# Splitting the last layer norm of a decoder layer over VectorE, ScalarE and GpSimd

## What is computed

```python
ALPHA = (2.0 * DEPTH) ** 0.25

def _layernorm(x, g, b):
    xf = x.astype(jnp.float32)
    mu = jnp.mean(xf, -1, keepdims=True)
    var = jnp.mean(jnp.square(xf - mu), -1, keepdims=True)
    return ((xf - mu) * lax.rsqrt(var + LN_EPS) * g + b).astype(x.dtype)
...
    x = _layernorm(ALPHA * x + (1 + g1) * (merged @ w_o), ln_mix_g, ln_mix_b)
    u2 = x * (1 + sc2) + sh2
    f = _hier_moe(u2.reshape(b * L, D), ...).reshape(b, L, D)
    x = _layernorm(ALPHA * x + (1 + g2) * f, ln_ffn_g, ln_ffn_b)
```

## Time and profile before

| | us |
|---|---|
| median of 3 runs | 2881.74 |
| lowest and highest of them | 2880.91, 2882.03 |
| the profiled execution | 2883.5 |
| its span, from the first to the last instruction | 2881.8 |
| TensorE busy | 2587.6 (90%) |
| VectorE busy | 1508.3 (52%) |
| ScalarE busy | 1051.6 (36%) |
| GpSimd busy | 425.4 (15%) |
| first landing of rows in the last stage | 2806.2 |
| last stage, from there to the end of the span | 75.6 |

### The profile page before, as it was taken

One profiled execution on the slowest core, in us unless ns is written; L12 is line 12 of the kernel. 1 busy time (PEld: TensorE's weight loads), 2 busy tenths in 40 slices (PEclk: granted clock), 3 DMA queues, 4 the chain that ended last, 5 costly groups with the idle time before them and its releaser, 6 DMA issues.

```text
span 2881.8 us, 34273 instructions
## 1 busy us (share of the span) xinstructions
PE 2587.6 (90%) x11876; PEld 1890.9 (66%) x11876; DVE 1508.3 (52%) x2374; ACT 1051.6 (36%) x1338; POOL 425.4 (15%) x261
## 2 busy tenths in 40 slices
PE   7999999999999976899999999999939999999970
PEld 2376666666666654677789998884427777777750
DVE  3332576766765767200012222115567888888869
ACT  0212645536446454200000000000017777777751
POOL 0000000000000001111034431110002233233220
PEclk8989999999999988899999999999959999999985
DMA  7721222222222211111111113121148999999963
GB/s 269 255 69 41 79 59 61 66 70 66 66 57 79 59 39 37 46 44 36 44 35 47 44 51 110 37 61 52 52 151 290 345 347 347 353 354 342 341 234 134
DMA packets 251191, 379.58 MB, mean 132 GB/s; under 512 B 17395, under 2 KB 167547, under 8 KB 251049
## 3 DMA queue, kind: packets, MB, share of 16 engines
q1 hardware_dynamic: 230272, 336.17, 35.3%
q0 software_dynamic: 11904, 26.15, 2.4%
q10 hardware_dynamic: 8928, 16.26, 1.8%
HBM read 356.21 MB, written 39.76 MB: 137 GB/s over the span
## 4 chain that ended last, share of the span: by engine, by line
PE 39%; issue 7%; DVE 6%; ACT 4%; DMA 2%; POOL 1%; DVEq 0%; ACTq 0%; POOLq 0%; SPq 0%
PE bank L1999 11%; PE bank L1961 5%; PE bank L1963 5%; PE bank L1962 5%; PE bank L2071 4%; ACT we_parts L1080 3%; PE bank L2135 2%; PE bank L2138 2%; PE bank L2139 2%; DVE we_parts L1574 1%; DMA rows_dram<-arena 1%; PE bank L2104 1%; DVE x_parts L1684 1%; ACT arena L1101 1%; PE bank L2145 1%
## 5 line engine op out<-in xcount | busy, mean ns | idle before, releaser
L1835 PE MATMUL bank<-u_whole,arena 128*128 128x344 f32 x2304 | 695.3, 458 | 0.0
L1835 PEld LDWEIGHTS bank<-u_whole,arena 128*128 128x128 f32 x2304 | 437.6, 193 | 221.6 <-issue 16.7
L1961 PE MATMUL bank<-u_parts,w_parts 128*128 128x344 f32 x960 | 313.8, 327 | 14.4 <-DVE u_parts L1434 7.3
L1574 DVE TENSOR_TENSOR we_parts<-u_whole,we_parts 128x2048 fp32r<-128x2048 f32 x129 | 295.1, 2287 | 57.5 <-ACT we_parts L1080 57.5
L1962 PE MATMUL bank<-u_parts,w_parts 128*128 128x344 f32 x960 | 308.6, 321 | 0.0
L1963 PE MATMUL bank<-u_parts,w_parts 128*128 128x344 f32 x960 | 308.5, 321 | 0.0
L1999 PE MATMUL bank<-arena 128*128 128x344 f32 x1056 | 307.8, 452 | 0.0
L1999 PEld LDWEIGHTS bank<-arena 128*128 128x128 f32 x1056 | 200.1, 190 | 101.8
L1080 ACT ACTIVATE we_parts<-u_whole 128x2048 fp32r<-128x2048 f32 x129 | 247.0, 1916 | 51.5 <-PE bank L2135 26.9
L2117 PE MATMUL bank<-we_parts,x_parts 128*128 128x512 f32 x512 | 210.0, 410 | 3.3 <-DVE we_parts L1574 1.9
L2119 PE MATMUL bank<-we_parts,x_parts 128*128 128x512 f32 x512 | 201.4, 393 | 0.0
(11 more groups left out here) (327 smaller groups left out, 3921.1 us busy)
## 6 DMA issues: line engine op xcount, KB each, us to landing
u_whole<-in_w_moe_dram SPq DMA_DIRECT2D x128, 1024.0 KB, 7.4
arena<-in_w_moe_dram SPq DMA_DIRECT2D x64, 1024.0 KB, 7.6
arena<-in_w_ada_dram SPq DMA_DIRECT2D x12, 2048.0 KB, 10.1
arena<-in_w_in_dram SPq DMA_DIRECT2D x48, 512.0 KB, 3.9
w_whole<-in_w_in_dram SPq DMA_DIRECT2D x40, 512.0 KB, 3.8
arena<-cum_dram ACTq DMA_DIRECT2D x62, 256.0 KB, 3.1
arena<-in_state_ssm_dram SPq DMA_DIRECT2D x16, 512.0 KB, 5.5
out_dram<-arena SPq DMA_DIRECT2D x16, 512.0 KB, 4.0
```

The lines of the kernel that those rows point to most:

```text
L1574: dve.tensor_tensor(w_los[v], wraw[slot], w_his[v].bitcast(F32), ALU.subtract).then_inc(wlo_ready, 1)
L1835: last = pe.matmul(banks[part][:, 0:SUB], wslot[u][:, k, :], uT[:, k, part * SUB:(part + 1) * SUB], start=(k == 0), stop=(k == KD - 1))
L1961: pe.matmul(out, w_hi[v][:, k, :], u_hi[:, k, at], start=(k == 0), stop=False)
```

## The change

The last three wide VectorE operations of a tile become three others. VectorE stops after mean and variance; later it works out two numbers for each row, 1 / std in `mv2[..., 3]` and - mean / std in `mv2[..., 0]` (`scale_of`). ScalarE applies them as scale and bias of one activation (`normed_rows`). GpSimd then multiplies with the weight row and adds the bias row, and raises `y_out`.

The order is set so: on VectorE, `scale_of(i - 1)` stands behind the combine of tile i; on ScalarE, `normed_rows(i - 1)` stands between the copy of tile i and its square root. The semaphores `mvar_ready` and `mstd_ready` are dropped, and `var_ready` and `std_ready` of the first normalisation are counted on; in the middle normalisation nothing else changes.

```diff
@@ gpsimd, behind its last scatter
+            pool.wait_ge(finw_landed, 64)
+            for i in range(TILES + 1):
+                rows = P if i < TILES else NS
+                x = fa[i % 3][0:rows, :]
+                pool.wait_ge(y_normed, i + 1)
+                st.did(pool.tensor_tensor(x, x, ffn_g[0:rows, :], ALU.mult))
+                st.settle()
+                pool.tensor_tensor(x, x, ffn_b[0:rows, :], ALU.add).then_inc(y_out, 1)
@@ scalar
+            def normed_rows(i):
+                rows = P if i < TILES else NS
+                act.wait_ge(scale_ready, i + 1)
+                act.activation(fa[i % 3][0:rows, :], fa[i % 3][0:rows, :], ACT.Identity, bias=mv2[0:rows, i % 2, 0:1],
+                               scale=mv2[0:rows, i % 2, 3:4]).then_inc(y_normed, 1)
+
             for i in range(TILES + 1):
...
                                scale=wts[0:rows, i:i + 1]).then_inc(f_scaled, 1)
-                act.wait_ge(mvar_ready, TILES + 2 + i)
+                if i >= 1:
+                    normed_rows(i - 1)
+                act.wait_ge(var_ready, 2 * TILES + 3 + i)
                 act.activation(mv2[0:rows, i % 2, 2:3], mv2[0:rows, i % 2, 1:2], ACT.Sqrt,
-                               bias=epsc[0:rows, :]).then_inc(mstd_ready, 1)
+                               bias=epsc[0:rows, :]).then_inc(std_ready, 1)
+            normed_rows(TILES)
@@ vector
+            def scale_of(i):
+                rows = P if i < TILES else NS
+                m = mv2[0:rows, i % 2, :]
+                dve.wait_ge(std_ready, 2 * TILES + 3 + i)
+                fin.did(dve.reciprocal(m[:, 3:4], m[:, 2:3]))
+                fin.settle()
+                dve.scalar_tensor_tensor(m[:, 0:1], m[:, 0:1], -1.0, m[:, 3:4], ALU.mult, ALU.mult).then_inc(scale_ready, 1)
+
             for i in range(TILES + 1):
...
                                                  ALU.mult, ALU.add))
+                if i:
+                    scale_of(i - 1)
                 fin.settle()
                 fin.did(dve.tensor_tensor(x, x, g2, ALU.mult))
...
                 fin.settle()
-                dve.bn_aggr(mv2[0:rows, i % 2, 0:2], stats2[0:rows, :]).then_inc(mvar_ready, 1)
-                dve.wait_ge(mvar_ready, TILES + 2 + i)
-                fin.did(dve.scalar_tensor_tensor(x, x, mv2[0:rows, i % 2, 0:1], ffn_g[0:rows, :], ALU.subtract,
-                                                 ALU.mult))
-                dve.wait_ge(mstd_ready, TILES + 2 + i)
-                fin.did(dve.reciprocal(mv2[0:rows, i % 2, 3:4], mv2[0:rows, i % 2, 2:3]))
-                fin.settle()
-                dve.scalar_tensor_tensor(x, x, mv2[0:rows, i % 2, 3:4], ffn_b[0:rows, :], ALU.mult,
-                                         ALU.add).then_inc(y_out, 1)
+                if i >= 2:
+                    dve.wait_ge(y_normed, i - 1)
+                dve.bn_aggr(mv2[0:rows, i % 2, 0:2], stats2[0:rows, :]).then_inc(var_ready, 1)
+            scale_of(TILES)
```

More of the change, by code:

```diff
@@ L379, in build @@
         x0_landed = [sem(f"x0_landed{i}") for i in range(2)]
-        wo_done, mvar_ready, mstd_ready, x0_used = sem("wo_done"), sem("mvar_ready"), sem("mstd_ready"), sem("x0_used")
+        wo_done, x0_used = sem("wo_done"), sem("x0_used")
         u2_ready, u2_turned, u2t_ready, logits_done = (sem("u2_ready"), sem("u2_turned"), sem("u2t_ready"),
@@ L399, in build @@
         f_scaled, y_out = sem("f_scaled"), sem("y_out")
+        scale_ready, y_normed = sem("scale_ready"), sem("y_normed")
         y_stored = [sem(f"y_stored{i}") for i in range(3)]
@@ L1051, in _ @@
                 rows = P if i < TILES else NS
-                act.wait_ge(mvar_ready, i + 1)
+                act.wait_ge(var_ready, TILES + 2 + i)
                 act.activation(mv2[0:rows, i % 2, 2:3], mv2[0:rows, i % 2, 1:2], ACT.Sqrt,
-                               bias=epsc[0:rows, :]).then_inc(mstd_ready, 1)
+                               bias=epsc[0:rows, :]).then_inc(std_ready, 1)
                 act.wait_ge(u2_turned, i + 1)
@@ L1526, in _ @@
                 st.settle()
-                dve.bn_aggr(mv2[0:rows, i % 2, 0:2], stats2[0:rows, :]).then_inc(mvar_ready, 1)
-                dve.wait_ge(mvar_ready, i + 1)
+                dve.bn_aggr(mv2[0:rows, i % 2, 0:2], stats2[0:rows, :]).then_inc(var_ready, 1)
+                dve.wait_ge(var_ready, TILES + 2 + i)
                 st.did(dve.scalar_tensor_tensor(x, x, mv2[0:rows, i % 2, 0:1], mix_g[0:rows, :], ALU.subtract,
                                                 ALU.mult))
-                dve.wait_ge(mstd_ready, i + 1)
+                dve.wait_ge(std_ready, TILES + 2 + i)
                 st.did(dve.reciprocal(mv2[0:rows, i % 2, 3:4], mv2[0:rows, i % 2, 2:3]))
```

## The result

The changed kernel takes 2892.14 us (median of 6 runs, 2889.89 to 2892.98) where the kernel before takes 2880.01 (median of 6 runs, 2874.90 to 2882.03). The ratio is 1.0043, with a 95% interval of 1.0030 to 1.0056, which is +8.6 to +16.1 us: slower, by 12.1 us. The forecast was +8.9.

What follows compares the result with a forecast made beforehand. The last stage was taken as bound by VectorE, nine tiles one behind the other at 8.0 us a turn. Start -0.9, turns +4.5 and tail +5.3 summed to +8.9 us: 2890.6 us against a median of 2881.74, range 2887 to 2898.

Steps and rivals of the forecast that it cites:

- The exclusion: Last stage: a GpSimd operation and a VectorE operation with two SBUF inputs exclude each other; handover gives back 0.14 us.
- The first rival: Last stage: GpSimd's multiplication gets ahead and holds the residual; turn 9.4 us, +15.2 us, 2896.9; chance 0.18.
- the narrow margin: Last stage: the residual is ready only 0.07 us ahead of GpSimd's multiplication, so their order could flip.
- GpSimd's 2.35 us: Last stage: each wide GpSimd operation with two full inputs takes 2.35 us, two a tile; lower end 1.89.
- The fourth rival: Last stage: exclusion, but 1.89 us for each GpSimd operation; loads bind at 8.05 a tile, +3.5 us, 2885.2; chance 0.07.
- The statistics: Last stage: VectorE's statistics, with one SBUF input, run free beside GpSimd's multiplication at 1.29 us.
- The second rival: Last stage: statistics are held by GpSimd too; turn 9.6 us, +17.5 us, 2899.3; chance 0.04.
- The turn: Last stage, one tile: 8.63 us against 8.0, combine held by GpSimd's addition; +4.5 us over seven turns.
- the cover of the loads: Last stage: late loads stay hidden behind the held combine by 0.24 us; loads half a microsecond longer add 1 us.
- Start and tail: Last stage: to the second residual's end -0.9 us; last residual to last addition 9.5 us for 4.2, +5.3.
- The store behind it is the same.: End of kernel: the store after the last addition is unchanged, so nothing is added there.
- The third rival: Last stage: nothing excludes anything; VectorE's turn 7.1 us until loads bind at 8.0, +2.5 us, 2884.2; chance 0.07.

## Why the prediction was right, step by step

**The exclusion** was there, and in the order that was forecast. The residual came ahead of the multiplication, by 0.18 us in seven of the eight tiles (0.29 in the first) and not 0.07: the ScalarE pass takes 1.24 us and not 1.13 as the copy. The first rival, which lived on the narrow margin, was further off than I thought. What did not hold is that the combine is held in every turn: with three buffers it was in two of seven, and by 0.27 us in a third. Nor does the exclusion alone decide the sign: without it, with four buffers, the stage was still 2.6 us longer than before. The Trainium skill, "ScalarE: Activation LUTs", section "What ACT_TABLE_LOAD costs", gives about 93 ns more for each pointer operand; the new pass has a pointer bias that the copy hasn't, and the 0.11 us between them are near to it.

**GpSimd's 2.35 us** measured 2.34 (2.33 on 8 rows). The fourth rival, with 1.89, is out.

**The statistics** stayed at 1.29 us beside the multiplication. The second rival is out, and the rule that the prediction cites from the Trainium skill for operations with one SBUF input agrees with this.

**The turn** of 8.63 measured 8.69, but for two causes that happened to add up. With loads out of the way it is 8.36, less than my 8.63: the reciprocal started before the combine's end and the narrow operation took 0.16 and not 0.23. And the cover of the loads, which I gave as 0.24 us, wasn't there: the copy at 2824.94 started 5.2 us after its loads were issued at 2819.72, and the next four copies 4.7 to 5.1 us after theirs, where I had taken 4.4. I had counted the landing from the first of the two issues, but the second is issued some 0.4 us later, and took up to 4.8 by itself. This term was mis-sized, by 0.3 to 0.8, and it changed what sets the turn: in four of the seven the combine waited for rows (8.6 to 9.4 us a turn), in three the exclusion set it (8.3 to 8.4). That the mean came out near 8.63 is luck.

**Start and tail**, -0.9 and +5.3, measured -1.0 and +5.1.

**What failed** is one sentence: "The store behind it is the same." The store is, but the program doesn't end with it. It ends when each engine has drained, and GpSimd, which had been done 83 us before the end, had become the last one. Those 5.2 us are missing from the sum: with them the forecast of the stage would have been +14.1, and it measured +14.2. Over whole runs the change measured +12.1, with an interval of +8.6 to +16.1. The +8.9, the +14.1 and the +14.2 all lie in it, +8.9 near its edge, so only the length of the stage tells them apart. The measured 2892.14 lies in the forecast range of 2887 to 2898, but just over the 2892 up to which the forecast itself was spanned; the range went on to 2898 for the first rival, which did not happen, and that the missing 5.2 us fitted into it is luck.

**The third rival**, no exclusion, was tried with four buffers only (6.96 us a turn); with three buffers it was not tried. How late the rows would come there without the exclusion is therefore open.

## What to carry to other kernels

Before work goes from VectorE to GpSimd, list the VectorE operations that will run beside it, and count those with two SBUF inputs: here 3.7 us of them and 4.7 us of GpSimd's work a turn could not overlap, and one operand in PSUM removed that. Even an operation on one column counts: one was held for 1.9 us. And look at which engine ends last: work moved to an engine that was done early also moves that engine's closing drain to the end, so its last share is better left to another.

## What the runs showed of the hardware that was not expected

- GpSimd's closing drain ended 7.0 us after its last work in all ten traces, whether that was a scatter (the kernel before), an operation on one column or a wide addition.
- A VectorE operation on a single column with two SBUF inputs took 2.10 us beside a GpSimd addition and 0.16 alone; with one tensor and one pointer scalar 0.21 beside it.
- The 128x1024 ScalarE pass with pointer scale and pointer bias took 1.24 us, with a pointer scale alone 1.13.
